# The second block of every expert gathered one expert ahead, and gathers that skip empty slots

## The reference

```python
def moe_ffn(h, w_router, b_router, w_gate, w_up, w_down):
    expert, weight = group_limited_route(h, w_router, b_router)   # 2 experts for each of 512 tokens
    ...                                                           # sort the 1024 (token, expert) pairs by expert,
                                                                  # pad every expert to blocks of 128 slots
    def expert_block(args):
        tok, e = args
        xb = h[tok]                                               # gather 128 token rows
        return (jax.nn.silu(xb @ w_gate[e]) * (xb @ w_up[e])) @ w_down[e]
    ...                                                           # weight the rows, add them to their tokens
```

## Time and profile before

| | us |
|---|---|
| median of 3 runs | 1515.39 |
| lowest and highest | 1515.05, 1520.22 |
| the profiled execution's own time | 1511.96 |
| its span, first to last instruction | 1510.3 |
| PE busy | 1394.2 (92%) |
| DVE busy | 970.8 (64%) |
| ACT busy | 720.6 (48%) |
| POOL busy | 208.8 (14%) |

### The profile page before, as it was taken

One profiled execution on the slowest core, in us unless ns is written; L12 is line 12 of the kernel. 1 busy time (PEld: TensorE's weight loads), 2 busy tenths in 40 slices (PEclk: granted clock), 3 DMA queues, 4 the chain that ended last, 5 costly groups with the idle time before them and its releaser, 6 DMA issues.

```text
span 1510.3 us, 18539 instructions
## 1 busy us (share of the span) xinstructions
PE 1394.2 (92%) x7113; PEld 1096.4 (73%) x7114; DVE 970.8 (64%) x929; ACT 720.6 (48%) x772; POOL 208.8 (14%) x200
## 2 busy tenths in 40 slices
PE   3999999999988899999969999999999899999593
PEld 1766777666677788888748787788777788888472
DVE  2426575323477799999781667632758889999183
ACT  2434355122155577777552536522325677776150
POOL 1000000000012123332220000000012123333021
PEclk9899999999999999999969999999998999999797
DMA  9665502766684899999842130132365999999265
GB/s 305 225 229 202 188 1 84 247 254 213 226 328 177 298 376 391 395 398 396 322 132 100 68 112 1 56 112 84 112 247 202 333 369 391 389 390 392 94 239 198
DMA packets 152802, 350.24 MB, mean 232 GB/s; under 512 B 10511, under 2 KB 12755, under 8 KB 152723
## 3 DMA queue, kind: packets, MB, share of 16 engines
q1 hardware_dynamic: 140018, 312.77, 56.4%
q0 software_dynamic: 12704, 36.38, 6.8%
HBM read 334.43 MB, written 23.61 MB: 237 GB/s over the span
## 4 chain that ended last, share of the span: by engine, by line
PE 73%; DVE 10%; DMA 7%; ACT 3%; DVEq 3%; issue 2%; SPq 1%; POOL 0%; POOLq 0%; ACTq 0%
PE PS L1132 14%; PE PS L1133 14%; PE PS L1134 14%; PE PS L1522 7%; PE PS L1526 7%; PE PS L1518 7%; PE PS L1066 3%; DMA ring<-in_w_ada 2%; ACT reg L887 2%; DVE ring_parts L2109 2%; PE PS L1506 2%; PE PS L1573 2%; DMA ring<-in_w_up 1%; PE PS L1531 1%; DMA reg<-y_rows 1%
## 5 line engine op out<-in xcount | busy, mean ns | idle before, releaser
L1132 PE MATMUL PS<-ring_parts 128*128 128x512 f32 (+1 forms) x704 | 277.3, 394 | 8.8 <-DVE hT_parts L1742 5.3
L2109 DVE TENSOR_TENSOR ring_parts<-ring,reg_parts 128x2048 fp32r<-128x2048 f32 x124 | 278.0, 2282 | 0.9 <-ACT reg_parts L990 0.9
L990 ACT ACTIVATE reg_parts<-ring 128x2048 fp32r<-128x2048 f32 x124 | 230.6, 1909 | 65.8 <-DMA ring<-in_w_down 31.9
L1734 DVE TENSOR_TENSOR ring_parts<-ring,ring_parts 128x2048 fp32r<-128x2048 f32 (+1 forms) x52 | 112.9, 2209 | 165.9 <-ACT ring_parts L808 165.8
L1132 PEld LDWEIGHTS PS<-ring_parts 128*128 128x128 f32 x704 | 133.8, 190 | 62.9 <-issue 30.7
L808 ACT ACTIVATE ring_parts<-ring 128x2048 fp32r<-128x2048 f32 (+1 forms) x52 | 93.3, 1845 | 170.3 <-DMA ring<-in_w_in 129.0
L2109 DVE TENSOR_TENSOR ring_parts<-ring,hT_parts 128x2048 fp32r<-128x2048 f32 x64 | 146.2, 2287 | 12.1 <-issue 11.0
L1134 PE MATMUL PS<-ring_parts 128*128 128x512 f32 x384 | 149.9, 390 | 0.0
L1133 PE MATMUL PS<-hT_parts,ring_parts 128*128 128x512 f32 x384 | 149.8, 390 | 0.0
L1526 PE MATMUL PS<-ring_parts,reg_parts 128*128 128x512 f32 x528 | 130.6, 389 | 0.0
L990 ACT ACTIVATE hT_parts<-ring 128x2048 fp32r<-128x2048 f32 x64 | 119.1, 1909 | 11.2 <-DMA ring<-in_w_gate 6.1
(11 more groups left out here) (327 smaller groups left out, 2368.4 us busy)
## 6 DMA issues: line engine op xcount, KB each, us to landing
ring<-in_w_up SPq DMA_DIRECT2D x32, 2048.0 KB
ring<-in_w_gate SPq DMA_DIRECT2D x32, 2048.0 KB, 11.1
ring<-in_w_down SPq DMA_DIRECT2D x32, 2048.0 KB
ring<-in_w_ada SPq DMA_DIRECT2D x40, 1024.0 KB, 5.2
ring<-in_w_in SPq DMA_DIRECT2D x16, 2048.0 KB, 8.4
ring<-in_w_ada SPq DMA_DIRECT2D x4, 2048.0 KB, 18.7
ring<-in_w_out SPq DMA_DIRECT2D x4, 2048.0 KB, 9.6
ring<-in_w_up_gla SPq DMA_DIRECT2D x2, 2048.0 KB
```

The source lines that it names most:

```text
L990: act.activation(w_high[part][:, cols], ring[:, 3 * k + part, cols], ACT.Copy).then_inc(w_hi[part], 1)
L1132: pe.matmul(out_, left[0], right[0], start=first, stop=False)
L1734: tt(ring_r[:, unit_slot(n), cols], w, ring_r[:, 2 + n % 2, cols].bitcast(F32), ALU.subtract).then_inc(lo_done, 1)
L2109: tt(ring_r[:, 3 * k + part, cols], ring[:, 3 * k + part, cols], w_high[part][:, cols].bitcast(F32), ALU.subtract).then_inc(w_lo[part], 1)
```

## The change

1. `gather_second_block(e)` is new. For every expert, without a test of the count, POOL gathers the column of block 1 into `o_xg` (semaphore `o_ahead`), one expert ahead: those of experts 0 and 1 before the ordinary gathers of experts 2 and 3, that of s + 1 in step s, behind the test of s and ahead of the scatter of s - 1. Each first waits for the one before it. The last scatter of a layer first waits for the last of them.
2. POOL's overflow body for block 1 no longer gathers. It copies the scatter column (`o_icur` + 2), waits for `o_ahead`, and copies the gather column (`o_icur` + 1), which now only signals. PE's body waits for `o_icur` at 3 per block. Blocks 2 and 3 gather as before and signal in the same way.
3. `gidx` is computed from `table`, so that an empty slot holds a row number beyond the end there too, and all gathers get a `bounds_check` that leaves it out. One cast and one copy go.
4. Two semaphores are merged, and counts follow.

```diff
--- before.py
+++ after.py
@@ -319,9 +319,8 @@
         orr_done = counted("gla_roots_ready", 1)
         o_done = counted("gla_o_read_then_roots_inverted_then_o_normed", 2 * GH + 1)
         INVERTED = GH + 1
-        qsq_done = counted("swa_squares_ready", 2)
+        qsq_done = counted("swa_squares_then_roots_ready", 3)
         qss_done = counted("swa_square_sums_ready", 2)
-        qrt_done = counted("swa_roots_ready", 1)
         rope_done = counted("swa_rotated", 1)
         qT_ready = counted("swa_qT_ready", NT)
         kT_ready = counted("swa_kT_ready", NT // 2)
@@ -363,7 +362,7 @@
         hot_done = counted("slot_columns_ready", TOPK * NT)
         tab_ready = counted("slot_table_ready", 1)
         idx_done = counted("gather_rows_ready", 1)
-        gcur_done = counted("gather_column_copied", E - 2)
+        gcur_done = counted("gather_column_copied", 2 * E - 2)
         dcur_done = counted("scatter_column_copied", E)
         xg_loaded = [counted(f"expert_tokens_gathered_{i}", 8 * E) for i in range(2)]
         t1_ready = counted("expert_tokens_transposed", E)
@@ -394,8 +393,9 @@
         pe_start = sem("condition_then_parameters_transposed")
         x_stored = sem("x_stored")
 
-        o_icur = sem("ovf_index_copied")
+        o_icur = sem("ovf_indices_copied_then_block_in_place")
         o_gath = sem("ovf_gathered")
+        o_ahead = counted("ovf_gathered_ahead", 16 * E)
         o_t1 = sem("ovf_tokens_transposed")
         o_t1c = sem("ovf_tokens_copied")
         o_xl = sem("ovf_tokens_low_ready")
@@ -596,6 +596,10 @@
 
             done = pool.alloc_register("pool_ovf")
             pool.reg_mov(done, 0)
+            later = pool.alloc_register("pool_ovf_later")
+            pool.reg_mov(later, 0)
+            placed = pool.alloc_register("pool_ovf_placed")
+            pool.reg_mov(placed, 0)
             number = pool.alloc_register("pool_wait_value")
 
             def in_register(value):
@@ -654,16 +658,32 @@
                 def first_gather(e):
 
                     pool.indirect_dma_start(out=xg[e], out_offset=None, in_=xs_rows[:, :],
-                                            in_offset=bass.IndirectOffsetOnAxis(ap=gidx[:, e * G4:e * G4 + 1].bitcast(U32), axis=0)).then_inc(xg_loaded[e], 16)
+                                            in_offset=bass.IndirectOffsetOnAxis(ap=gidx[:, e * G4:e * G4 + 1].bitcast(U32), axis=0),
+                                            bounds_check=SEQ - 1, oob_is_err=False).then_inc(xg_loaded[e], 16)
 
                 def gather(e, k):
 
                     pool.tensor_copy(icur[:, k:k + 1], gidx[:, bass.ds(e * G4, 1)]).then_inc(gcur_done, 1)
-                    value = in_register(at(gcur_done, l, e - 1))
+                    value = in_register(at(gcur_done, l, 2 * e - 2))
                     pool.wait_ge(pool_consts, 9)
                     pool.wait_ge(gcur_done, value)
                     pool.indirect_dma_start(out=xg[k], out_offset=None, in_=xs_rows[:, :],
-                                            in_offset=bass.IndirectOffsetOnAxis(ap=icur[:, k:k + 1].bitcast(U32), axis=0)).then_inc(xg_loaded[k], 16)
+                                            in_offset=bass.IndirectOffsetOnAxis(ap=icur[:, k:k + 1].bitcast(U32), axis=0),
+                                            bounds_check=SEQ - 1, oob_is_err=False).then_inc(xg_loaded[k], 16)
+
+                def gather_second_block(e, copied):
+
+                    if not isinstance(e, int) or e > 0:
+                        value = in_register(at(o_ahead, l, 16 * e))
+                        pool.wait_ge(pool_consts, 9)
+                        pool.wait_ge(o_ahead, value)
+                    pool.tensor_copy(icur[:, 6:7], gidx[:, bass.ds(e * G4 + 1, 1)]).then_inc(gcur_done, 1)
+                    value = in_register(at(gcur_done, l, copied))
+                    pool.wait_ge(pool_consts, 9)
+                    pool.wait_ge(gcur_done, value)
+                    pool.indirect_dma_start(out=o_xg, out_offset=None, in_=xs_rows[:, :],
+                                            in_offset=bass.IndirectOffsetOnAxis(ap=icur[:, 6:7].bitcast(U32), axis=0),
+                                            bounds_check=SEQ - 1, oob_is_err=False).then_inc(o_ahead, 16)
 
                 def scatter(e, k, stored):
 
@@ -682,13 +702,29 @@
 
                 def overflow(e):
                     def body(b, n):
-                        pool.tensor_copy(icur[:, 4:5], gidx[:, bass.ds(e * G4 + b, 1)]).then_inc(o_icur, 1)
-                        pool.tensor_copy(icur[:, 5:6], table[:, bass.ds(e * G4 + b, 1)]).then_inc(o_icur, 1)
-                        value = in_register(2 * n)
-                        pool.wait_ge(pool_consts, 9)
-                        pool.wait_ge(o_icur, value)
-                        pool.indirect_dma_start(out=o_xg, out_offset=None, in_=xs_rows[:, :],
-                                                in_offset=bass.IndirectOffsetOnAxis(ap=icur[:, 4:5].bitcast(U32), axis=0)).then_inc(o_gath, 16)
+                        if b == 1:
+                            pool.tensor_copy(icur[:, 5:6], table[:, bass.ds(e * G4 + b, 1)]).then_inc(o_icur, 2)
+                            value = in_register(at(o_ahead, l, 16 * e + 16))
+                            pool.wait_ge(pool_consts, 9)
+                            pool.wait_ge(o_ahead, value)
+                            pool.tensor_copy(icur[:, 4:5], gidx[:, bass.ds(e * G4 + b, 1)]).then_inc(o_icur, 1)
+                            pool.reg_add(placed, placed, 3)
+                        else:
+                            pool.tensor_copy(icur[:, 4:5], gidx[:, bass.ds(e * G4 + b, 1)]).then_inc(o_icur, 1)
+                            pool.tensor_copy(icur[:, 5:6], table[:, bass.ds(e * G4 + b, 1)]).then_inc(o_icur, 1)
+                            pool.reg_add(placed, placed, 2)
+                            value = pool.snap(placed, min_val=1, max_val=1 << 14)
+                            pool.wait_ge(pool_consts, 9)
+                            pool.wait_ge(o_icur, value)
+                            pool.indirect_dma_start(out=o_xg, out_offset=None, in_=xs_rows[:, :],
+                                                    in_offset=bass.IndirectOffsetOnAxis(ap=icur[:, 4:5].bitcast(U32), axis=0),
+                                                    bounds_check=SEQ - 1, oob_is_err=False).then_inc(o_gath, 16)
+                            pool.reg_add(later, later, 16)
+                            value = pool.snap(later, min_val=16, max_val=1 << 14)
+                            pool.wait_ge(pool_consts, 9)
+                            pool.wait_ge(o_gath, value)
+                            pool.tensor_copy(icur[:, 7:8], icur[:, 4:5]).then_inc(o_icur, 1)
+                            pool.reg_add(placed, placed, 1)
                         value = n
                         pool.wait_ge(pool_consts, 9)
                         pool.wait_ge(o_y, value)
@@ -710,13 +746,17 @@
                 first_gather(0)
                 pool.wait_ge(xg_loaded[0], at(xg_loaded[0], l, 16))
                 first_gather(1)
+                gather_second_block(0, 1)
                 gather_next(0, 0)
                 overflow(0)
+                gather_second_block(1, 3)
                 gather_next(1, 1)
 
                 def step(s, k, stored, more=True):
 
                     overflow(s)
+                    if not isinstance(s, int) or s < E - 1:
+                        gather_second_block(s + 1, 2 * s + 3 if more else E + s)
                     scatter(s - 1, 1 - k, stored)
                     if more:
                         gather_next(s + 1, 1 - k)
@@ -733,6 +773,9 @@
                 pool.wait_ge(y_stored[1], at(y_stored[1], l, 8 * E - 16))
                 for t in range(NT):
                     pool.dma_start(yc[t][:, 0, :], chosen_rows(t, 0)).then_inc(yc_first, 16)
+                value = in_register(at(o_ahead, l, 16 * E))
+                pool.wait_ge(pool_consts, 9)
+                pool.wait_ge(o_ahead, value)
                 scatter(E - 1, 1, E // 2 - 1)
                 value = in_register(at(x2_done, l, NT))
                 pool.wait_ge(pool_consts, 9)
@@ -839,7 +882,7 @@
                         act.wait_ge(qss_done, at(qss_done, l, 1))
                     act.activation(sqt, qk[:, 2 * i:2 * i + 2, :, :].rearrange("p t h d -> p (t h d)"), ACT.Square).then_inc(qsq_done, 1)
                 act.wait_ge(qss_done, at(qss_done, l, 2))
-                act.activation(qss[:, :, :], qss[:, :, :], ACT.Sqrt, scale=1.0 / HD, bias=eps).then_inc(qrt_done, 1)
+                act.activation(qss[:, :, :], qss[:, :, :], ACT.Sqrt, scale=1.0 / HD, bias=eps).then_inc(qsq_done, 1)
                 for t in range(NT):
                     act.wait_ge(v_ready, at(v_ready, l, t + 1))
                     act.activation(v[:, t, :], PS[:, in_bank(Q_V + t), :], ACT.Copy).then_inc(v_done, 1)
@@ -1575,7 +1618,7 @@
 
                 def overflow(e, pair, k, evacuated):
```

(12 more changed lines are left out.)

## The result

| | before | after | ratio (95% interval) |
|---|---|---|---|
| median of 7 runs each | 1516.51 | 1504.62 | 0.9917 (0.9893 to 0.9942) |
| median in a second comparison (18 and 6 runs) | 1516.63 | 1500.66 | 0.9896 (0.9875 to 0.9917) |
| the profiled execution, its span | 1511.96, 1510.3 | 1502.02, 1500.1 | |

The change makes the kernel faster by 0.8 to 1.0%, 12 to 16 us. Single runs of either kernel spread over 5 to 14 us, so differences of one or two microseconds are read from the traces, not from medians. In the first pair of profiled executions the gain is 9.9 us, in a second pair (1513.98 before, 1500.38 after) 13.6.

A forecast was written before the change was run, and what follows sets the result against it. PE was taken to set the pace, busy 17.70 us of a 17.7 us loop step. Gains of 7.9 + 0.7 + 1.4 = 10.0 us gave 1502.0 profiled and, from the median 1515.39, 1505.4 us; range 1500 to 1511.

The forecast's parts named there:

- The stall: Second block of expert 13, layer 1: PE's wait for its gather cut from 10.3 to 2.4 us, gaining 7.9.
- The clock: Behind that wait: transposes regain 0.7 us of full clock; gate matmuls still start at half clock, 2.8 us not won.
- rival 1: Second block's transposes keep the clock, so the gate's 2.8 us are won too: 12.8 in all, 1502.6; chance 0.22.
- The first gathers: Start of each layer: shorter routing chain and fewer rows landing gain 0.1 + 0.8 + 0.5 = 1.4 us.
- What is added, at nothing: POOL's extra wait, copy and gather per expert, 1.9 to 5.9 us per step, covered by its idle before the scatter.
- Bytes bring nothing: Full expert loop: some 8.9 MB fewer gathered bytes save no time by themselves, since PE is busy 17.70 of 17.70.
- The signs: Expected profile: PE wait of 2 to 3 us released by POOL's copy, 32 more gathers, 17.7 us steps, 27.5 MB queue.
- Rival 2: Entering the overflow code costs PE time the idle had covered; if 3 of 7.9 us go, 1508.4; chance 0.12.
- rival 3: Gather ahead not there in time, or empty indirect DMA slow, so the second block's stall stays: 1514; chance 0.08.
- Rival 4: Loop steps: POOL's added copy and issue hold VectorE, which becomes the bound, 0.8 us per step: 1527; chance 0.06.

The follow-up runs named there:

- direct_clock: Changed kernel, with PE waiting for the second block's gather itself and 14 spare products behind that block's transposes: 1511.93 us, 0.9966 of the kernel before.
- direct_wait: Changed kernel, with PE's second-block body waiting for the gather's own semaphore instead of POOL's copy: 1503.71 us, 0.9911 of the kernel before.
- keep_clock: Changed kernel plus spare products in PE's overflow body, 8 before its wait and 14 behind its transposes: 1510.89 us, 0.9965 of the kernel before.
- tested_wide: Changed kernel, gathering ahead only after a count test, PE waiting for the gather itself, five wide spare products in block 1: 1498.05 us, 0.9884 of before.
- pool_busy: Changed kernel with five more small POOL copies ahead of each second block's copy: 1505.83 us, 0.9907 of the kernel before.
- ahead_full: Changed kernel with empty slots gathered again, so the gather ahead moves 128 rows for every expert: 1537.72 us, 1.0148 of the kernel before.

## Why the prediction was right

It forecast 1505.4 (1500 to 1511); 1504.62 was measured, and in the profiles 10.0 was forecast and 9.94 found. The agreement to 0.1 us is luck: the second pair of profiles gives 13.6. What is not luck is the largest term.

- **The stall**, 7.9: measured 8.7 (8.1 in the second pair, idles of 10.08 and 2.00 us). The mechanism was as told: the gather landed unseen, POOL's copy is late next. POOL's copy ended 1.5 us behind PE's up product and woke PE within 0.05; I had given 0.7 us to a wait that costs nothing when it is satisfied.
- **The clock**, 0.7 for the transposes and nothing for the gate: measured 0.9 and nothing (6.43 against 6.39). `direct_clock` shows that rival 1's prize was real, and `direct_wait` that it takes more than the idle ahead of the transposes: with only the 2.46 us of idle behind the transposes the clock still fell. `keep_clock` and `tested_wide` show that a clock saved there can be lost in the down product.
- **The first gathers**, 1.4: measured 0.5, the term that was mis-sized. From the first instruction on the table to the tokens it is 7.36 us before and 7.05 after in layer 0, 7.46 and 7.29 in layer 1. The rows left out bring almost nothing: from the end of POOL's issue to the tokens of layer 0 it was 3.12 us with 128 rows and is 2.95 with 35. My slope of 2.6 us per 512 KB came from whole transfers of 128 rows by POOL's plain path, and did not carry over. The fit of the Trainium skill's "DMA: Bandwidth & Descriptors", anatomy of one DMA on the GpSimd path, that I had set beside it, an estimated 0.87 us for 93 rows, is not borne out either: 0.17 us were found.
- **What is added, at nothing**: right in the loop, where `pool_busy` shows the cover to be as wide as claimed, wrong by 1.2 to 1.9 us from the tokens of expert 15 of layer 1 to the end (55.7 and 56.0 us after, 54.1 and 54.5 before).
- **Bytes bring nothing**: wrong as far as it went beyond the full loop steps, which are still of 17.70 us. Skipping alone is worth 6.5 us (3.6 to 9.4) by the ratio. One to two of them sit in the first steps of layer 0, where PE stands idle at its jumps; where the rest sits stays open. The prediction saw those idles and used them for a rival, but did not ask what shortens them.
- **The signs**: the queue's bytes, the releaser of the wait, the loop steps and the slow gate came as told. The net number of added gathers is 31, not 32, and the first wait for tokens fell to 1.35 us and not 2.4, but it was 1.61 in the second profile of before, so it was no sign of anything.
- Rival 2 (code fetched on entering the body) did not come, rival 3 neither. Rival 4's effect, VectorE held up by POOL, exists in small, at one place. The total was right in part by luck, because terms of about 1 to 2 us cancelled: more from the stall and the first steps, less from the first gathers and the tail; and 1.2 us of the trace's gain lie ahead of the routing table, which the change does not touch.

## What to carry to other kernels

Work that only a rare case needs can be done ahead for every case, if it moves no bytes when it is not needed and stands on an engine with idle time ahead of its next deadline; without the skipping the same reordering cost 1.5%. A test in front of it served as well here. When the wait is gone, look at which signal the consumer now hangs on, and hang it on the data itself. And look at the code that an unlikely branch jumps over as a cost of the likely path: here the third and fourth blocks' code, on all engines, was worth 7 to 10 us, beside 12 to 16 of the whole change. Whoever fills a hole with spare work to hold the clock has to look at the holes behind it, too.

## What the runs showed of the hardware

- Jumping over code costs PE idle time without a releaser: 0.3 to 3.6 us each at the first jumps, 5.1 and 5.3 us behind the second block once its code was longer. Before the token transposes these idles are none with 44 packets of instructions, 6.5 to 8.2 us in eight profiles with 54, 12.7 in the ninth (`ahead_full`, where DMA is the bound), 8.2 and 10.5 with 55, 17.1 with 58 and 16.5 with 61. In a steady loop, after the first passes, they don't come again: steps of 17.70.
- Spare products behind the eight transposes kept the granted clock at 1.00 through the gate; without them it fell to half in the idle of 2.46 us there, in the changed kernel, where 1.55 us of idle stand ahead of the transposes, and in `direct_wait`, where none does. What half the clock costs is 2.8 us on sixteen matmuls of 512 columns (6.4 against 3.6).
- A skipped slot moves 4 bytes and not 4096, but it is still a packet: with skipping alone POOL's queue has the same 12704 packets for 27.48 MB as before for 36.38; those of 4096 bytes fall from 8832 to 6656, those of 4 bytes rise from 3712 to 5888.
- An indirect DMA whose slots are all empty completes, and holds POOL for 1.03 us in the median, as one with rows does (1.04).
- The bound makes POOL start later: 0.89 us after the index is there, against 0.28, in the first gather of layer 0. In both its issue ends about 1.0 us behind VectorE's first subtraction, so nothing seems lost by it.
